# First mLSTM gates worked out among the input projection's tiles, decay products removed, and twelve unused products ahead of the prompt recurrence

## The chip, the cores and the metric

One core of one Trainium2 chip runs the whole program. The metric is the device time of one execution in microseconds (us). Five engines work side by side: TensorE (PE in the profile; PEld is its weight load), VectorE (DVE), ScalarE (ACT), GpSimd (POOL) and SyncE (SP), which here only issues DMAs. Each runs its own instruction stream in order and waits on semaphores; a DMA issue (SPq, ACTq) occupies the queue of the engine that issues it.

## The reference, cut to what matters

The step has an mLSTM layer (mixer A), a feed-forward, shared keys and values, a second attention layer and another feed-forward, for one prompt of 1024 frames and eight running streams of 16 frames. All is fp32. What the change touches is the start of mixer A:

```python
q, k, v, o, ig, fg = jnp.split(xn @ w_in, [...], axis=-1)   # 512, 512, 1024, 1024, 8, 8 columns
li = soft_cap(ig + b_i)                  # 15 * tanh(z / 15), per head and frame
lf = log_sigmoid(soft_cap(fg + b_f))
b = jnp.cumsum(lf, axis=-1)              # within a chunk
dmat = where(causal, b[..., :, None] - b[..., None, :] + li[..., None, :], -inf)
m_t = maximum(b + m, max(dmat)); g = exp(b + m - m_t)
s = einsum('bhtd,bhsd->bhts', q, k) * exp(dmat - m_t[..., None])     # the decay
num = g * einsum('bhvd,bhtd->bhtv', c, q) + einsum('bhts,bhsv->bhtv', s, v)
...
c_new = g_c * c + einsum('bhsv,bhsd->bhvd', ws * v, k)               # the state, chunk to chunk
```

## The kernel before, in words

The 1152 frames (1024 of the prompt, 128 of the running streams) are nine tiles of 128. Each stage is a block of five instruction streams; a stage begins when all five of the one before have ended.

**w_in** (function `linear`, lines 368 to 610). Weights arrive on SP's queue in quarters of a 512-column block (L433); POOL splits each quarter into a high and a low part (L61, L456); TensorE makes three products per 128 rows of the contraction and tile (L499 to L501), `t` over nine tiles inside `b` over six blocks; ScalarE copies each finished tile out of PSUM and issues its store to the scratch `qkvo` in DRAM. Behind the sixth block stand the first gates: 72 products of 128x384 (L510 to L512), whose rows go to DRAM (L440).

**Gates** (`mlstm_gates`, L1255 to L1390). The gate rows come back as 8 partitions (one per head) by 1152 frames, and VectorE and ScalarE work out tanh, log-sigmoid, the cumulative sum, the running maximum and the factors per frame in one chain. TensorE turns the results (L1377 to L1384). Nothing else runs meanwhile.

**Prompt recurrence** (`mlstm`, from L1393; its tiles are named mprompt). Eight tiles, each with four pairs of heads. Per pair TensorE makes: a turn of the next tile (L1554, three per tile), the decay of the pair after next (L1563, L1565, L1566: five products, the mask and the cumulative rows spread over 128 partitions by one-hot weights), the next pair's scores (L1577), the numerator (L1604, L1612) and the state's update (L1620). VectorE adds the frame's own gate to the decay (`argument`, L1756), ScalarE takes its exponential (L1676), VectorE multiplies it into the scores (L1764), ScalarE copies the numerator out (L1711) and VectorE scales the state (L1798). At the second pair of a tile VectorE divides the previous tile's output (L1769 to L1774). SP loads two tiles ahead (L1471 queries and keys, L1475 values). In the second tile ScalarE's queue issues thirteen loads of the running streams' states (L1686 to L1690).

**Running recurrence** (mrun, the same function with one tile), and then a chain of projections that begins with w_out. TensorE's order there is written out by hand: per pair the turn, the decay of the pair after next, the next pair's scores, then this pair's numerator and state.

Of the kernel before, what the change touches and what calls it, by code (L numbers as in the profile page):

```python
# [367 lines left out]
def linear(nc, g, xth, xtl, tag, w, segments, gates=None, **source):  # L368
    BANKS = 3
    wv = w.rearrange("(k p) n -> p k n", p=P)  # L370
    QUARTERS = 4
    HK = KC // QUARTERS
    nb = sum(n for _, n, _, _ in segments)
    with Scope(nc, tag) as s:
        raw = s.sb("raw", [P, 2, HK, CB])
        wh, wl = s.sb("wh", [P, 2, KC, CB], fp32r), s.sb("wl", [P, 2, KC, CB], fp32r)
        if segments[0][2] != "residual":
            stage = s.sb("stage", [P, BANKS, CB])
        normed = [m for _, _, m, _ in segments if isinstance(m, tuple)]
        loaded = [s.sem(f"w_loaded{i}") for i in range(2)]  # L380
        w_split, high_sem = s.sem("w_split"), s.sem("w_high")
        psum_ready, stage_ready = s.sem("psum_ready"), s.sem("stage_ready")
        psum_used = [s.sem(f"psum_used{i}") for i in range(len(segments))]
        stored = [s.sem(f"stored{i}") for i in range(BANKS)]
        psum = [s.ps(f"y{i}", [P, CB]) for i in range(BANKS)]
        if normed:
            gain_small, gain = s.sb("gain_small", [P, B_HD]), s.sb("gain", [P, B_HD])
            squares, ss, rms = s.sb("squares", [P, CB]), s.sb("ss", [P, A_H]), s.sb("rms", [P, A_H])
            gain_loaded, square_done, mean_done, root_done = s.sem("gain_loaded"), s.sem("square"), s.sem("mean"), s.sem("root")
        chain_sem = s.sem("chain")  # L390
        tok = s.brief("tok", [P, Activations.SLOTS, D]) if gates else s.sb("tok", [P, Activations.SLOTS, D])
        if gates:

            gh, gl = s.sb("gh", [P, KC, P], fp32r), s.sb("gl", [P, KC, P], fp32r)
        xt = Activations(nc, g, s, xth, xtl, tok=tok, psum=[s.ps(f"xt{i}", [P, CB]) for i in range(2)], **source)
        if gates:
            g_col, g_n, g_parts, g_bias = gates
            g_raw = s.sb("g_raw", [P, KC, g_n])
            g_out = stage[0:g_n, :, :].rearrange("p a n -> p (a n)")
            g_loaded, g_split, g_ready, g_copied, g_stored = (s.sem(n) for n in ("g_loaded", "g_split", "g_ready", "g_copied", "g_stored"))  # L400
            g_psum = [s.ps(f"g{i}", [P, THIRD]) for i in range(3)]
            if g_bias is not None:
                g_add, g_add_loaded = s.sb("g_add", [g_n, 1]), s.sem("g_add_loaded")

        def each_segment(engine, body, chain=None, when=lambda m: True):

            b0 = 0
            for n, (col0, blocks, mode, target) in enumerate(segments):
                if when(mode):
                    start = chain.n if chain else 0  # L410
                    pairs = blocks // 2
                    run(engine, pairs, lambda i: body(n, i, b0), chain)
                b0 += blocks

        with nc.Block() as block:

            @block.sync
            def _(sp):
                if gates and g_bias is not None:
                    sp.dma_start(g_add[:, :], g_bias.rearrange("(h o) -> h o", o=1)).then_inc(g_add_loaded, 16)  # L420
                if normed:
                    sp.dma_start(gain_small[:, :], normed[0][1].to_broadcast((P, B_HD))).then_inc(gain_loaded, 16)

                xt.load_gain(sp)

                def load(n, i, b0):
                    for par in range(2):
                        b = b0 + 2 * i + par
                        col = segments[n][0] + (2 * i + par) * CB
                        for h in range(QUARTERS):  # L430
                            if h >= 2 or not below(b, 1):
                                wait(sp, w_split, QUARTERS * b + h - 1)
                            sp.dma_start(raw[:, h % 2], wv[:, h * HK:(h + 1) * HK, bass.ds(col, CB)]).then_inc(loaded[h % 2], 16)  # L433

                each_segment(sp, load)
                if gates:
                    sp.dma_start(g_raw[:, :, :], wv[:, :, g_col:g_col + g_n]).then_inc(g_loaded, 16)
                    wait(sp, g_copied, 3)
                    for dst, a, b in g_parts:
                        sp.dma_start(dst, g_out[:, a:b]).then_inc(g_stored, 16)  # L440
                    wait(sp, g_stored, 16 * len(g_parts))

            @block.gpsimd
            def _(pool):
                def split(n, i, b0):
                    for par in range(2):
                        b = b0 + 2 * i + par
                        for h in range(QUARTERS):
                            wait(pool, loaded[h % 2], (2 * b + h // 2) * 16 + 16)
                            if not below(b, 2):  # L450

                                wait(pool, psum_ready, (b - 1) * NT)
                            ks = slice(h * HK, (h + 1) * HK)
                            round_high(pool, g, wh[:, par, ks], raw[:, h % 2]).then_inc(high_sem, 1)
                            wait(pool, high_sem, QUARTERS * b + h + 1)
                            pool.tensor_tensor(wl[:, par, ks], raw[:, h % 2], f32(wh[:, par, ks]), ALU.subtract).then_inc(w_split, 1)  # L456
                            if below(b, 1):
                                xt.scale_gates(pool, h)
                        if below(b, 1):
                            for t in range(QUARTERS, NT):  # L460
                                xt.scale_gates(pool, t)

                each_segment(pool, split)
                if gates:
                    wait(pool, g_loaded, 16)
                    wait(pool, xt.transposed, 2 * NT)
                    pool.memset(f32(gh[:, :, :]), 0.0).then_inc(g_split, 1)
                    pool.memset(f32(gl[:, :, :]), 0.0).then_inc(g_split, 1)
                    wait(pool, g_split, 2)
                    pool.tensor_copy(gh[:, :, 0:g_n], g_raw[:, :, :]).then_inc(g_split, 1)  # L470
                    wait(pool, g_split, 3)
                    pool.tensor_tensor(gl[:, :, 0:g_n], g_raw[:, :, :], f32(gh[:, :, 0:g_n]), ALU.subtract).then_inc(g_split, 1)

            @block.tensor
            def _(pe):
                def products(n, i, b0):
                    for par in range(2):
                        b = b0 + 2 * i + par
                        for t in range(NT):
                            bank = t % BANKS  # L480
                            if below(b, 1):
                                if t == 0:
                                    xt.transpose(pe, 0)
                                    xt.transpose(pe, 1)
                                else:
                                    xt.transpose(pe, t + 1)
                                pe.wait_ge(xt.low_done, 2 * t + 2)
                            if t < BANKS and b0 == 0 and par == 0 and below(i, 1):
                                pass
                            elif t < BANKS and par == 0 and below(i, 1):  # L490

                                pe.wait_ge(psum_used[n - 1], NT * segments[n - 1][1] - BANKS + t + 1)
                            else:
                                pe.wait_ge(psum_used[n], (b - b0) * NT + t - BANKS + 1)
                            for k in range(KC):
                                if t == 0 and k % HK == 0:
                                    pe.wait_ge(w_split, QUARTERS * b + k // HK + 1)
                                xs = slice(t * P, (t + 1) * P)
# [15 lines left out]

            @block.scalar
            def _(act):
                xt.start_act(act)
                xt.high(act, 0)
                xt.high(act, 1)

# [88 lines left out]

class NextTiles:


# [765 lines left out]

# [1411 lines left out]
```

## Time and profile before

| what | us |
|---|---|
| median of three runs | 3531.0 (3496.63, 3531.0, 3543.12) |
| profiled execution | 3529.51 (its span 3528.1) |
| TensorE busy | 3242.7 (92%) |
| mean granted TensorE clock | 0.943 of full speed |
| w_in, from its first product to its last | 17.54 to 342.85 |
| gates stage | 346.4 to 395.0 |
| prompt recurrence, first DMA issue to last state update | 396.2 to 550.1 |
| running recurrence | 562.7 to 626 |

The granted clock is given as a share of full speed: 1.00 is the upper of TensorE's two levels (2.4 GHz), 0.50 the lower (1.2 GHz). Busy time is not useful time: a product at the lower level is busy for twice as long. In a timeline row the bracket says how long the engine had been idle, and for what.

### The profile page before, as it was taken

The numbers are of one execution on the slowest core, as the hardware profiler recorded it, in microseconds if no ns is written. First come the engines' busy times: TensorE is split into PE (matmuls) and PEld (weight loads), VectorE is DVE, ScalarE is ACT, GpSimd is POOL, SyncE is SP. The second block draws the span as 40 slices with busy tenths as digits, with TensorE's granted clock in tenths as the row PEclk, the third lists the DMA queues.
The fourth block names the chain that finished last, engine by engine and source line by source line (L and its number), as shares of the span: only waits on it lengthen the run. The fifth ranks groups of instructions, "written<-read, shape, count | busy, mean of one in ns | idle before, by whom it ended". The sixth has DMA issues, their size and how long they took to land. (4 is left out here: it accounts for less than half of the span.)

```text
span 3528.1 us, 43496 instructions
## 1 busy us (share of the span) xinstructions
PE 3242.7 (92%) x17307; PEld 2797.5 (79%) x17307; DVE 1208.5 (34%) x1913; ACT 608.5 (17%) x1212; POOL 1204.2 (34%) x692
## 2 busy tenths in 40 slices
PE   7998497599999999998999969997779999999999
PEld 6887375479999999986878846665568999999998
DVE  3000433852223332236425135552334233332323
ACT  3111122220000000002111114443313000000000
POOL 4340121452333233423424125662143332234320
PEclk9999567799999999999999969998989999999999
DMA  4221221511111111101222124325651111111111
GB/s 146 96 85 41 58 81 52 173 57 34 60 48 36 36 36 59 36 31 60 93 76 93 63 67 107 93 61 179 220 187 36 48 36 36 36 53 42 48 36 54
DMA packets 177733, 254.44 MB, mean 72 GB/s; under 512 B 33748, under 2 KB 115304, under 8 KB 177608
## 3 DMA queue, kind: packets, MB, share of 16 engines
q1 hardware_dynamic: 137016, 183.19, 16.7%
q10 hardware_dynamic: 38672, 64.27, 5.2%
q0 software_dynamic: 1920, 5.24, 0.4%
q8 instruction: 87, 1.43, 0.2%
q14 instruction: 38, 0.31, 0.0%
HBM read 194.23 MB, written 50.44 MB: 69 GB/s over the span
## 5 line engine op out<-in xcount | busy, mean ns | idle before, releaser
L1081 PE MATMUL A_bank<-A_xth,A_w 128*128 128x384 f32 x1056 | 353.0, 334 | 0.0
L1081 PE MATMUL B_bank<-B_xth,B_w 128*128 128x384 f32 x1056 | 353.0, 334 | 0.0
L1083 PE MATMUL B_bank<-B_xtl,B_w 128*128 128x384 f32 x1056 | 352.9, 334 | 0.0
L1083 PE MATMUL A_bank<-A_xtl,A_w 128*128 128x384 f32 x1056 | 352.9, 334 | 0.0
L1082 PE MATMUL A_bank<-A_xth,A_w 128*128 128x384 f32 x1056 | 352.8, 334 | 0.0
L1082 PE MATMUL B_bank<-B_xth,B_w 128*128 128x384 f32 x1056 | 352.8, 334 | 0.0
L61 POOL TENSOR_TENSOR A_w1h<-A_raw_a,g_one 128x1024 fp32r<-128x1024 f32 (+1 forms) x31 | 79.8, 2574 | 500.1 <-PE A_bank L1109 323.4
L1181 DVE TENSOR_TENSOR g_x<-B_bank,g_x 128x512 f32<-128x512 f32 x198 | 136.9, 692 | 209.7 <-PE B_bank L1109 209.7
L1181 DVE TENSOR_TENSOR g_x<-A_bank,g_x 128x512 f32<-128x512 f32 x198 | 136.2, 691 | 201.9 <-PE A_bank L1109 201.9
L1081 PEld LDWEIGHTS A_bank<-A_xth,A_w 128*128 128x128 f32 x1056 | 198.3, 188 | 0.6 <-issue 0.2
L1081 PEld LDWEIGHTS B_bank<-B_xth,B_w 128*128 128x128 f32 x1056 | 198.3, 188 | 0.6 <-issue 0.2
L1082 PEld LDWEIGHTS A_bank<-A_xth,A_w 128*128 128x128 f32 x1056 | 198.3, 188 | 0.4
L1082 PEld LDWEIGHTS B_bank<-B_xth,B_w 128*128 128x128 f32 x1056 | 198.3, 188 | 0.4
L1083 PEld LDWEIGHTS B_bank<-B_xtl,B_w 128*128 128x128 f32 x1056 | 198.3, 188 | 0.0
L1083 PEld LDWEIGHTS A_bank<-A_xtl,A_w 128*128 128x128 f32 x1056 | 198.3, 188 | 0.0
L499 PE MATMUL w_in_y<-w_in_wh,A_xth 128*128 128x512 f32 x432 | 171.3, 396 | 7.5 <-POOL w_in_wl L456 7.5
L2100 POOL TENSOR_TENSOR fprompt_acc<-fprompt_acc,fprompt_prob 128x512 f32<-128x512 f32 (+3 forms) x160 | 152.4, 952 | 60.7 <-ACT fprompt_prob L2286 44.8
L61 POOL TENSOR_TENSOR B_w1h<-B_raw_a,g_one 128x2048 fp32r<-128x2048 f32 (+1 forms) x15 | 48.1, 3209 | 360.6 <-PE B_bank L1109 323.4
L501 PE MATMUL w_in_y<-w_in_wh,A_xtl 128*128 128x512 f32 x432 | 170.1, 394 | 0.0
L500 PE MATMUL w_in_y<-w_in_wl,A_xth 128*128 128x512 f32 x432 | 170.0, 394 | 0.0
L61 POOL TENSOR_TENSOR A_w<-A_raw_a,g_one 128x1024 fp32r<-128x1024 f32 x42 | 88.7, 2112 | 235.2 <-PE A_bank L873 80.3
L1107 PE MATMUL A_bank<-A_w1h,A_w1l 128*128 128x512 f32 x396 | 156.7, 396 | 12.2 <-issue 7.3
(470 smaller groups left out, 6915.4 us busy)
## 6 DMA issues: line engine op xcount, KB each, us to landing
frun_v<-in_cache_v_dram SPq DMA_DIRECT2D x8, 2048.0 KB, 8.9
qkvo<-w_in_stage ACTq DMA_DIRECT2D x54, 256.0 KB, 2.0
w_in_raw<-in_w_in_a_dram SPq DMA_DIRECT2D x24, 512.0 KB, 3.7
A_raw_b<-in_w_gu_dram SPq DMA_DIRECT2D x11, 1024.0 KB
A_raw_a<-in_w_down_dram SPq DMA_DIRECT2D x11, 1024.0 KB, 4.8
B_raw_b<-in_w_gu_dram SPq DMA_DIRECT2D x11, 1024.0 KB
B_raw_a<-in_w_down_dram SPq DMA_DIRECT2D x11, 1024.0 KB, 4.8
A_raw_a<-in_w_gu_dram SPq DMA_DIRECT2D x10, 1024.0 KB
```

The source lines that it names most:

```text
L61: return pool.tensor_tensor(out, in_, ones, ALU.mult)
L499: pe.matmul(psum[bank][:, :], xth[:, k, xs], wh[:, par, k], start=(k == 0), stop=False)
L500: pe.matmul(psum[bank][:, :], xth[:, k, xs], wl[:, par, k], start=False, stop=False)
L501: ins = pe.matmul(psum[bank][:, :], xtl[:, k, xs], wh[:, par, k], start=False, stop=(k == KC - 1))
L1081: pe.matmul(banks[j][:, :], h[:, f, k], xth[:, k, self.thirds[j]], start=(k == 0), stop=False)
L1082: pe.matmul(banks[j][:, :], l[:, f, k], xth[:, k, self.thirds[j]], start=False, stop=False)
L1083: ins = pe.matmul(banks[j][:, :], h[:, f, k], xtl[:, k, self.thirds[j]], start=False, stop=(k == KC - 1))
L1107: pe.matmul(self.yp[c][:, :], self.hh[:, f, ts], self.dh[:, f, cs], start=(f == 0), stop=False)
L1181: dve.tensor_tensor(xs, self.yp[c][:, :], xs, ALU.add).then_inc(self.added, 1)
L2100: pool.tensor_tensor(to, to, new, ALU.add).then_inc(summed, 1)
```

## The change

`linear` is gone; w_in uses the class `Linear` that four later projections already used, unrolled. It is given a block number at which the gate products stand: 1 here, so they come after block 0 and ahead of block 1. The gate weights are loaded first on SP's queue. A new class `MlstmGates` is a guest of w_in: it works on 64 partitions (head and chunk) by 144 frames, and puts its ScalarE, TensorE and DMA work at fixed (block, tile) places; its cumulative rows go to DRAM. In the recurrences SP loads those rows, broadcast to 128 partitions, for each tile, and VectorE builds the argument from them, the frame's gate and the mask. The five decay products per pair, their PSUM banks and the five casts ahead of them are gone. Ahead of the prompt recurrence's first turn stand twelve products whose result nothing reads.

```diff
 class Linear:
     def sp(self, sp):
+            for a, b, bias in self.g_bias:
+                sp.dma_start(self.g_add[a:b, :], bias).then_inc(self.g_add_loaded, 16)
         for b, (n, bl) in enumerate(self.blocks):
-            if b == 1 and self.gates:
+            if self.gates and b == self.g_block - 2 + (self.g_block == 1):
                 sp.dma_start(self.g_raw[:, :, :], ...).then_inc(self.g_loaded, 16)
...
+            if self.gates and b == self.g_block:
+                sp.wait_ge(self.g_copied, 3)
+                for dst, c0, c1 in self.g_parts:
+                    sp.dma_start(dst, self.g_out[:, c0:c1]).then_inc(self.g_stored, 16)
+                if self.guest:
+                    sp.wait_ge(self.g_stored, 16 * len(self.g_parts))
+                    self.guest.sp_in(sp)
     def pe(self, pe):
-            if last and self.gates:
+            if self.gates and b == self.g_block:
                 self.gate_products(pe)
...
+                if self.guest:
+                    self.guest.pe(pe, b, t)
+class MlstmGates:
+    ROWS = A_H * NP
+    ACT_AT = {(1, 5): "tanh", (1, 7): "exp", (2, 0): "log", (2, 8): "exps"}
+    PE_AT = {(2, 3): "link", (2, 5): "back", (3, 2): "turn"}
...
 def mlstm(...):
+        bb = s.sb("bb", [P, SLOTS, A_H, P])
+        warm = s.ps("warm", [P, CB])
+        WARM = 12
                     sp.dma_start(qk[:, slot], qkvo[t, :, 0:A_V0]).then_inc(qk_loaded[slot], 16)
                     if not below(i, SLOTS):
+                        wait(sp, arg_done, (i - SLOTS + 1) * A_PAIRS)
+                    cols = b_d[:, bass.ds(i * P, P)].rearrange("(o h) n -> o h n", o=1)
+                    sp.dma_start(bb[:, slot], cols.to_broadcast((P, A_H, P))).then_inc(b_loaded[slot], 16)
...
-                def bias(i, slot, j):
-                    pe.matmul(bank[:, :, :], g.ident_r[:, :], mask_r[:, :, :], start=True, stop=False)
-                    for e in range(2):
-                        pe.matmul(bank[:, e, :], g.sel_r[:, 2 * j + e, :], g.Bh[:, cols], start=False, stop=False)
-                        ins = pe.matmul(bank[:, e, :], g.sel_r[:, 2 * j + e, :], g.Bl[:, cols], start=False, stop=(e == 1))
-                    ins.then_inc(bias_ready, 1)
...
-                pe.wait_ge(rounded, 1 if running else 5)
+                if not running:
+                    for n in range(WARM):
+                        pe.matmul(warm[:, :], g.ident[:, :], g.x[:, n % NP, 0:CB], start=True, stop=True)
...
                 def argument(i, slot, j):
-                    dve.wait_ge(bias_ready, i * A_PAIRS + j + 1)
-                    dve.tensor_tensor(arg[:, j], pb[j % 2][:, :, :], spread(tokc[:, slot, KIND_A, 2 * j:2 * j + 2], P), ALU.add).then_inc(arg_done, 1)
+                    if j == 0:
+                        dve.wait_ge(b_loaded[slot], loads(i, slot))
+                    for e in range(2):
+                        h = 2 * j + e
+                        ins = dve.scalar_tensor_tensor(arg[:, j, e, :], bb[:, slot, h, :], tokc[:, slot, KIND_A, h:h + 1], mask[:, e, :], ALU.add, ALU.add)
+                    ins.then_inc(arg_done, 1)
...
-            mlstm_gates(nc, g, gates_d, A["b_i_a"], A["b_f_a"], A["state_m"], m_prompt, m_sample)
+                              gates=(A_O0 + A_H * A_V, 2 * A_H, [...], bias, 1, 3), own=own, guest=gates)
```

On TensorE, before, the gates' last small products are followed by the first turns and the first decay products:

```order
L1377 MATMUL mgates_tok<-g_ident,mgates_en 128x8
L1382 MATMUL mgates_small<-mgates_gend,A_pair_sel 128x8 x4
L1383 MATMUL mgates_small<-mgates_diag,A_ones 128x64
L1384 MATMUL mgates_small<-g_ident,mgates_gend 8x8
L1278 UNCONDITIONAL_BRANCH
L1526 UNCONDITIONAL_BRANCH
L1554 MATMUL mprompt_turn<-g_ident,mprompt_qk 128x128 x8
L1554 MATMUL mprompt_turn<-g_ident,mprompt_qg 128x128 x4
L1563 MATMUL mprompt_bias<-mprompt_mask_r,A_ident_r 128x256
```

With the change, the last products of w_in are followed by the unused ones, and the first pairs have no decay (mprompt_bias):

```order
L642 MATMUL A_bank<-A_w1h,A_xth 128x512
L643 MATMUL A_bank<-A_w1l,A_xth 128x512
L644 MATMUL A_bank<-A_w1h,A_xtl 128x512
L969 UNCONDITIONAL_BRANCH
L1339 UNCONDITIONAL_BRANCH
L1435 MATMUL mprompt_warm<-g_x,g_ident 128x512 x12
L1367 MATMUL mprompt_turn<-g_ident,mprompt_qk 128x128 x8
L1367 MATMUL mprompt_turn<-g_ident,mprompt_qg 128x128 x4
L1378 MATMUL mprompt_scores<-mprompt_qt,mprompt_kt 128x128 x4
L1405 MATMUL mprompt_num_p<-mprompt_v,mprompt_st 128x129 x2
L1413 MATMUL mprompt_num_p<-mprompt_ct,mprompt_qgt 128x129 x2
L1421 MATMUL mprompt_state<-mprompt_wsv,mprompt_k 64x129 x2
```

The gates stage between the two has gone from this place. On SP, before, the w_in weights come first behind the norm's gain, and the gate weights last:

```order
L232 DMA w_in_x_gain<-in_g_mix_dram 128x1024
L433 DMA w_in_raw<-in_w_in_a_dram 128x2x512 x8
L95 UNCONDITIONAL_BRANCH
L433 DMA w_in_raw<-in_w_in_a_dram 128x2x512 x8
L95 REGISTER_ALU
L95 COMPARE_AND_BRANCH
L433 DMA w_in_raw<-in_w_in_a_dram 128x2x512 x8
L437 DMA w_in_g_raw<-in_w_in_a_dram 128x8x16
L440 DMA mlstm_gates_rows<-w_in_stage 16x1152
```

With the change three small loads are ahead of them, and the gates' stores, reloads and old maxima stand between the second and the third block's weights:

```order
L232 DMA A_gain<-in_g_mix_dram 128x1024
L560 DMA A_w_in_g_add<-in_b_i_a_dram 8x1
L560 DMA A_w_in_g_add<-in_b_f_a_dram 8x1
L563 DMA A_gate_raw<-in_w_in_a_dram 128x8x16
L570 DMA A_raw_a<-in_w_in_a_dram 128x2x512 x8
L578 DMA mlstm_gates_prompt<-A_raw_b 16x1024
L578 DMA mlstm_gates_running<-A_raw_b 16x128
L1073 DMA A_gain<-mlstm_gates_prompt 64x128
L1073 DMA A_gain<-mlstm_gates_running 64x16
L1073 DMA A_gain<-mlstm_gates_prompt 64x128
L1073 DMA A_gain<-mlstm_gates_running 64x16
L1075 DMA A_m_prev<-in_state_m_dram 8x1 x8
```

So a transfer of 64 KB in pieces of 16 columns now stands ahead of the first weights, and a wait of SP's stands ahead of the third block's.

## Rows read from the trace of the kernel before

**Rows 1.** Windows by stage: start:end, length, busy us of each engine, granted clock, DMA share, GB/s.

```profile
36.10:330.00 293.90, 293.90 (x1324) 243.91 (x1323) 18.87 (x29) 46.19 (x82) 84.86 (x43) 1.00 0.25 84
343.00:401.00 58.00, 6.21 (x47) 6.05 (x47) 34.52 (x46) 12.20 (x11) 5.82 (x15) 0.53 0.08 17
401.00:510.60 109.60, 104.15 (x461) 77.94 (x461) 30.76 (x83) 24.52 (x55) 23.05 (x16) 0.50 0.34 89
510.60:550.10 39.50, 39.11 (x308) 29.18 (x307) 20.11 (x54) 14.57 (x34) 12.10 (x8) 1.00 0.23 80
```

**Rows 2.** Windows inside the prompt recurrence, same columns.

```profile
460.00:480.00 20.00, 20.00 (x93) 14.80 (x91) 6.31 (x17) 4.86 (x11) 4.41 (x3) 0.50 0.13 41
```

**Rows 3.** Timeline, end of w_in and small gate products: start, length, engine, line, operation.

```profile
342.51 0.34 PE L512 MATMUL w_in_g<-A_xtl,w_in_gh 128*128 128x384 f32 x1
343.39 0.35 SPq L440 DMA_DIRECT2D mlstm_gates_rows<-w_in_stage  x1
346.38 0.34 SPq L1282 DMA_DIRECT2D mgates_li<-mlstm_gates_rows  x1
391.86 1.85 PE L1382 MATMUL mgates_small<-mgates_gend,A_pair_sel 8*128 8x8 f32 x8
```

**Rows 4.** Timeline, start of the prompt recurrence.

```profile
396.20 0.38 SPq L1471 DMA_DIRECT2D mprompt_qk<-qkvo  x1
401.03 1.09 PE L1554 MATMUL mprompt_turn<-g_ident,mprompt_qk 128*128 128x128 f32 x4 [6.79 <-DMA mprompt_qk<-qkvo]
402.89 1.09 PE L1554 MATMUL mprompt_turn<-g_ident,mprompt_qk 128*128 128x128 f32 x4 [0.78 <-ACT mprompt_qt L1681]
411.60 1.23 PE L1604 MATMUL mprompt_num_p<-mprompt_v,mprompt_st 128*128 128x129 f32 x4
```

**Rows 5.** Timeline, one pair of heads at the lower clock level.

```profile
477.61 0.58 PE L1563 MATMUL mprompt_bias<-mprompt_mask_r,A_ident_r 128*128 128x256 f32 x1
479.15 0.80 PE L1577 MATMUL mprompt_scores<-mprompt_qt,mprompt_kt 64*128 64x128 f32 x4
479.88 1.23 PE L1604 MATMUL mprompt_num_p<-mprompt_v,mprompt_st 128*128 128x129 f32 x4
485.44 0.80 PE L1604 MATMUL mprompt_num_p<-mprompt_v,mprompt_st 128*128 128x129 f32 x2
```

**Rows 6.** Timeline, last tile, upper clock level; its last pairs have no decay products.

```profile
540.69 0.39 PE L1563 MATMUL mprompt_bias<-mprompt_mask_r,A_ident_r 128*128 128x256 f32 x1
541.59 0.49 PE L1577 MATMUL mprompt_scores<-mprompt_qt,mprompt_kt 64*128 64x128 f32 x4
542.01 0.71 PE L1604 MATMUL mprompt_num_p<-mprompt_v,mprompt_st 128*128 128x129 f32 x4
544.47 1.22 DVE L1774 TENSOR_TENSOR mprompt_hout<-mprompt_num,mprompt_den 128x1024 f32<-128x1024 f32 x1
544.77 0.71 PE L1604 MATMUL mprompt_num_p<-mprompt_v,mprompt_st 128*128 128x129 f32 x4
546.90 0.68 PE L1604 MATMUL mprompt_num_p<-mprompt_v,mprompt_st 128*128 128x129 f32 x4
```

**Rows 7.** Timeline, ScalarE's queue while it issues the state's loads.

```profile
432.22 9.44 ACTq L1690 DMA_DIRECT2D A_cold<-in_state_c_dram  x8
442.54 1.20 PE L1604 MATMUL mprompt_num_p<-mprompt_v,mprompt_st 128*128 128x129 f32 x4 [3.87 <-ACT mprompt_num L1711]
```

**Rows 8.** Timeline, plain fp32 products 128x512 in the running recurrence.

```profile
610.44 1.02 PE L1653 MATMUL mrun_state<-mrun_wsk,A_own 128*8 128x512 f32 x2
611.39 1.13 PE L1663 MATMUL mrun_turn<-mrun_km,mrun_wsv 128*128 128x512 f32 x2
616.37 2.07 PE L1663 MATMUL mrun_turn<-mrun_km,mrun_wsv 128*128 128x512 f32 x2 [0.20 <-DVE A_cold L1826]
```

**Rows 9.** Timeline, VectorE in the recurrence: the argument now, and a fused operation.

```profile
541.70 0.42 DVE L1756 TENSOR_TENSOR mprompt_arg<-mprompt_bias,mprompt_tokc 128x256 f32<-128x256 f32 x1 [0.55 <-PE mprompt_bias L1566]
543.57 0.35 DVE L1798 SCALAR_TENSOR_TENSOR mprompt_ct<-mprompt_ct,mprompt_gcc,mprompt_state 128x129 f32<-128x129 f32 x1 [0.96 <-PE mprompt_state L1620]
```

More of the change, by code:

```diff
@@ L727, in __init__ @@
         self.bank = [s.ps(f"bank{i}", [P, CB]) for i in range(8)]
+        self.gate_raw = self.raw_b[:, T_ALL:T_ALL + n].rearrange("p (k n) -> p k n", k=KC)
         self.hh = self.w1l[:, T_ALL:(1 + FG) * T_ALL]
         self.w = [(self.w0[:, 0, :], self.w0[:, 1, :]), (self.w1h[:, :], self.w1l[:, :])]
+class FirstMemory:
+    def __init__(self, s):
+        self.xth, self.xtl = s.sb("xth", [P, KC, T_ALL], fp32r), s.sb("xtl", [P, KC, T_ALL], fp32r)
+        self.gate_raw = s.sb("gate_raw", [P, KC, 2 * A_H])
+        self.gate_w = [s.sb(f"gate_w{i}", [P, KC, 2 * A_H], fp32r) for i in range(2)]
+        self.raw_b, self.raw_a = s.sb("raw_b", [P, 2 * D]), s.sb("raw_a", [P, 2 * D])
+        pairs = [[s.sb(f"w{i}{part}", [P, KC * CB], fp32r) for part in "hl"] for i in range(2)]
+        self.w = [(h[:, :], l[:, :]) for h, l in pairs]
+        self.wide, self.gain = s.sb("wide", [P, Linear.BANKS * CB]), s.sb("gain", [P, D])
+        self.bank = [s.ps(f"bank{i}", [P, CB]) for i in range(8)]
 class Linear:
@@ L771, in __init__ @@
             self.g_out = mem.raw_b[0:self.g_n, 0:T_ALL]
-            self.g_psum = [mem.bank[5 + j][:, 0:THIRD] for j in range(3)]
+            self.g_psum = [b[:, 0:THIRD] for b in mem.bank[g_bank:g_bank + 3]]
             names = ("loaded", "add_loaded", "split", "ready", "copied", "stored")
@@ L806, in sp @@
                     sp.dma_start(self.gain_small[:, :], self.normed[0][1].to_broadcast((P, B_HD))).then_inc(self.gain_loaded, 16)
-        if self.then:
-            self.then.load_gain(sp)
-        if self.gates:
-            sp.wait_ge(self.g_copied, 3)
-            for dst, a, b in self.g_parts:
-                sp.dma_start(dst, self.g_out[:, a:b]).then_inc(self.g_stored, 16)
+            if b == self.nb - 1 and self.then:
+                self.then.load_gain(sp)
+            if self.gates and b == self.g_block:
[6 more added lines that the diff above has]
+        if self.guest:
+            self.guest.sp_out(sp)
     def sp_end(self, sp):
@@ L820, in pool @@
             par = b % 2
-            if b == 2 and self.gates:
+            if self.gates and b == self.g_block - 1:
                 pool.wait_ge(self.g_loaded, 16)
@@ L902, in act @@
             last = b == self.nb - 1
-            if last and self.gates:
-                act.wait_ge(self.g_add_loaded, 16)
+            if self.gates and b == self.g_block:
+                act.wait_ge(self.g_add_loaded, 16 * len(self.g_bias))
                 for j in range(3):
@@ L1398, in mlstm @@
+def mlstm(nc, g, qkvo, b_d, h_d, running, c_out, n_out, state_c=None, state_n=None):
     tag = "mrun" if running else "mprompt"
@@ L2681, in build @@
     qkvo = scratch("qkvo", (NT, P, A_O0 + A_H * A_V))
-    gates_d = scratch("mlstm_gates_rows", (2 * A_H, T_ALL))
+    gates_d, b_d = ([scratch(f"{name}_{part}", (rows, n)) for part, n in (("prompt", SEQ), ("running", T_ALL - SEQ))]
+                    for name, rows in (("mlstm_gates", 2 * A_H), ("mlstm_cum", A_H)))
     h_d = scratch("mlstm_h", (NT, P, D))
@@ L2701, in build @@
         setup(nc, g)
-        with Scope(nc, "A1") as s:
-            xth, xtl = s.sb("xth", [P, KC, T_ALL], fp32r), s.sb("xtl", [P, KC, T_ALL], fp32r)
-            linear(nc, g, xth, xtl, "w_in", A["w_in_a"][0],
-                   [(0, 4, "store", lambda b, t: qkvo[t, :, bass.ds(b * CB, CB)]),
-                    (A_O0, 2, "sigmoid", lambda b, t: qkvo[t, :, bass.ds(A_O0 + b * CB, CB)])],
-                   gates=(A_O0 + A_H * A_V, 2 * A_H, [(gates_d, 0, T_ALL)], None), kind="norm", gain_row=A["g_mix"][0:1, :], x_arrives=True)
@@ L2745, in build @@
                           (D, 2, "store", rows(v_prompt, v_sample))],
-                         gates=(2 * D, B_H, [(fgates_p, 0, SEQ), (fgates_s, SEQ, T_ALL)], A["b_f_b"]), made=xkv, raw_free=(ffn0.down_split, ffn0.G),
+                         gates=(2 * D, B_H, [(fgates_p, 0, SEQ), (fgates_s, SEQ, T_ALL)], [(0, B_H, A["b_f_b"].rearrange("(h o) -> h o", o=1))], 3, 5), made=xkv, raw_free=(ffn0.down_split, ffn0.G),
                          w_free=([(ffn0.up_ready, ffn0.ALL)], [(ffn0.down_ready, ffn0.G * ffn0.NY), (xkv.transposed, 2 * NT)]),
```

571 lines of the change are left out of this document (188 added, 383 removed).

## The prediction

> **What bounds the kernel now.** I read the windows by stage first, then the timeline at both ends of the stages that the change touches, and then single pairs of the recurrence at either clock level. The windows show three different limits. From 36.1 to 330 us TensorE is busy for all of 293.90 us at granted clock 1.00, so w_in ends when its products end, and whatever moves in among them is added [rows 1]. From 343 to 401 us TensorE does 6.21 us of work in 58: the gates' chain on VectorE is the end there, with the stage changes and the first load [rows 1]. The prompt recurrence then keeps TensorE busy for 104.15 of 109.60 us at clock 0.50, and for 39.11 of 39.50 at 1.00 [rows 1]. So in the recurrence TensorE is the bound at both levels, and the lower level is nearly three quarters of it. The reader should see that the kernel loses time here twice: 58 us with no products, and 110 us of products at half speed.
>
> **Against what the sum is made.** The profiled execution took 3529.5 us, 1.5 below the median of 3531.0; the three runs lie up to 47 apart, so a part of this stretch, such as the moment at which the clock comes back, may differ from run to run. I name the time at which the last state update of the prompt recurrence ends, 550.1 now [rows 1], and take everything behind it as moved by the same amount.
>
> **Start of w_in.** Three small loads are issued on SP ahead of the first weights. An issue costs about 0.35 us [rows 3], so 1.1 us at least; at most the first weights are held for as long as the first load of the recurrence takes from issue to use, 4.83 us (396.20 to 401.03) [rows 4]. I take 2.5, nearer the issues, because the load is an eighth of that one's size. The Trainium skill ("DMA: Bandwidth & Descriptors", section "Specifications") gives 512 B as the least piece at line rate, and the moved load has pieces of 64 B; no run here shows the load alone, and by that the delay would lie in the upper half of these bounds.
>
> **Gate products and their chain.** The 72 products are the same in number and length, only earlier: nothing won or lost on TensorE. Thirteen small products and transposes of the new class are added among w_in's. The nearest row is 1.85 us for four small products at the lower level (eight records) [rows 3], 0.46 each, so 0.23 at the upper: 13 of them are 3.0 us; bounds 1 (hidden in the pipeline) and 6. The chain on VectorE (34.5 us busy before [rows 1]) lies beside products now: VectorE does 18.87 us in the 293.90 of w_in, ScalarE 46.19 [rows 1]. Its cover is some 240 us of products behind block 0; the third block's weights wait on SP for the gates' store, with most of a block in hand. If that cover failed, the third block would start late; that is a rival below. So the last product of w_in ends at 342.85 + 2.5 + 3.0 = 348.4 (342.51 + 0.34 is its end now [rows 3]).
>
> **The exit of the stage.** From that end to the next stage's first DMA issue is 3.5 us now (342.85 to 346.38) [rows 3]; the last store is larger in the new order, so I take 3.8. The recurrence begins at 352.2, where it now has its first issue at 396.20 [rows 4]: 44 us go.
>
> **The twelve unused products.** A plain fp32 product 128x512 starts 0.95 us after the one before at the upper level (610.44 to 611.39) and lasts 2.07 at the lower, against 1.13 [rows 8]. Twelve are 11.4 us, or at most 22.8. The first load hides 4.83 of it [rows 4], so they cost 6.6 us net, 18 at the worst, and can give back only through the clock. First turn at 363.6 instead of 401.03.
>
> **The opening.** From first turn to first numerator is 10.6 us now, at the lower level, with two pairs' decay [rows 4]. A pair's decay is 1.54 us there (477.61 to 479.15) [rows 5], so 7.5 are left; part of it is ScalarE's copies between turns, which follow no TensorE clock. I take 6.7 at the upper level, 7.5 at the lower.
>
> **A tile of the recurrence.** At the upper level a pair without a turn takes 2.76 us (542.01 to 544.77), of which decay is 0.90 (540.69 to 541.59) [rows 6]: 1.86 remain. Four of these and three turns of about 0.4 (1.09 long at the lower level, with its drain [rows 4]) are 8.6 us. VectorE's own work per pair grows: two fused operations 128x128 in place of one of 0.42 over 256 columns. The nearest row is the fused 128x129 at 0.35 [rows 9], so 0.70 against 0.42; with the scores' product and the state it needs about 1.5 of the pair's 1.86. That fits, except where the previous tile's output is divided: that lump holds a 1.22 us operation, and the one row that shows a pair without decay behind the lump gives 2.13 instead of 1.86 (544.77 to 546.90) [rows 6], with the old argument. With the slower one I add 1.4 per tile (bounds 0.3, from this row, and 2.4, no overlap at all): 10.0 per tile, 80 for eight.
>
> **The stall on ScalarE's queue.** The eight state loads hold it for 9.44 us [rows 7]; the exponentials and copies stand behind them. TensorE idles 3.87 us [rows 7] now, because it had work left at the lower level. Faster products use that work up sooner: I take 8.5 (bounds 3.9 and 9.4).
>
> **The clock.** It is at 1.00 when w_in ends, and after 343 the mean of 0.53 over 58 us says that it fell within about 3.5 us of TensorE's last work [rows 1]. So it will fall in the stall, and perhaps just as the unused products begin. I add 5 us for such stretches (bounds 0 and 35, the next paragraph's rival). By the Trainium skill ("TensorE: Matmul & The Clock Gate", section "HAM oscillation — how this bites in real kernels") it is waits between bursts that throttle TensorE again; that speaks against relying on the unused products, since the stall comes after them. But it would also have the unbroken products of 460 to 480 us at the upper level, and the row says 20.00 of 20.00 us busy at 0.50 [rows 2]; there the measurement decides, and a busy engine is no promise of the upper level.
>
> **The sum.** 363.6 + 6.7 + 80 + 8.5 + 5 = 463.8 for the recurrence's end, against 550.1: 86.3 us. The running recurrence loses four decay groups of at most 1.54; part lies under ScalarE's copies, so 3.5 of 6.2. Together 89.8: 3529.5 - 89.8 = **3440 us**, 2.6% under the median.
>
> **Rivals.** (1) **The lower level stays** through the recurrence, as it did for 110 us under a fully busy engine [rows 1, 2]. A tile is then four pairs of 5.56 (479.88 to 485.44, one of them without its turn) less four decays of 1.54 [rows 5], about 15.3; 7.5 + 8 x 15.3 + 5 of stall = 135, end 499, so 55 us less than now: 3475. For it: rows 2. Against it: the same stream did run at 1.00 for its last 39.5 us [rows 1], and without the decay products, which use 8 rows of the array, what remains is denser. Chance 0.20. (2) **The clock is never lost**, or the lump hides: 3428, chance 0.05. (3) **The gates hold up w_in**: a step of the chain is late at its place and the third block's weights come late; 15 us more, 3455; chance 0.04. (4) **Slower: the loads bound the tiles.** SP's queue now holds queries and keys, the broadcast rows, and values, with two tiles in flight, and values are asked for only when the last numerator of the tile before is done. What is won outside the tiles is 37 + 4 us, so the kernel becomes slower when a tile takes over (149 + 41 - 7.5)/8 = 22.8 us. The first load lands in 4.8 us [rows 4] and DMA share is 0.34 [rows 1], so the broadcast would have to make it over three times as long; at 25 us a tile 3547. Chance 0.03. That the change doesn't do what it says is unlikely: the decay products and the gates stage are absent from the order.
>
> **Numbers.** 3440 with chance 0.68, its own range 3420 to 3460. The range 3418 to 3478 takes in rivals 1 to 3 and the bounds of stall, lump and clock. What a measurement here can tell from no change is about 2%, so faster means below 3460: 0.73, from the main case, (2), most of (3) and a little of (1), whose half-way forms lie on the border; same 0.24; slower 0.03.
>
> **What would show it.** Right: first turn near 364, granted clock near 1.00 in the second half of the recurrence, pairs of 1.9 to 2.5 us, one gap of 8 us on TensorE behind the state loads, recurrence over by 465. Wrong: a gap of TensorE between blocks of w_in; pairs of 3.4 us or more at 0.50; TensorE waiting for DMA at the head of tiles.

## The result, and the profile after

The changed kernel takes 3480.25 us (median of 13 runs, 3467.97 to 3485.37) against 3541.3 for the kernel before (13 runs, 3496.63 to 3553.72): the ratio is 0.9856, 95% interval 0.9827 to 0.9885. It is faster by 1.4%, clear of the noise, but by less than the 2% that the prediction took as the least that a measurement here tells from no change; 2.6% were forecast, and the time lies 2 us above the forecast range. The ratios in this document are worked out from averages that leave out executions in a slower state, as some of the kernel before are, so they differ a little from the quotient of the medians. The profiled execution took 3479.06 us against 3529.51.

The windows by stage of the changed kernel answer to [rows 1]; the columns are the same:

```profile
36.10:330.00 293.90, 293.90 (x1352) 239.77 (x1351) 43.95 (x82) 52.28 (x92) 83.58 (x39) 1.00 0.25 82
346.00:362.00 16.00, 12.03 (x25) 5.21 (x25) 2.18 (x6) 0.60 (x1) 2.12 (x5) 0.89 0.65 143
362.00:369.00 7.00, 2.99 (x21) 2.00 (x19) 0.95 (x3) 3.97 (x7) 3.38 (x2) 0.87 0.72 169
369.00:466.00 97.00, 84.13 (x398) 57.93 (x396) 38.03 (x111) 23.87 (x57) 22.30 (x15) 0.50 0.50 126
466.20:483.30 17.10, 11.85 (x97) 8.24 (x96) 11.33 (x27) 5.09 (x12) 5.36 (x4) 1.00 0.41 115
483.30:504.00 20.70, 19.82 (x96) 13.63 (x96) 9.87 (x25) 5.53 (x14) 4.10 (x5) 0.50 0.06 26
```

The gates' 58 us are gone: w_in is full as before, and 16 us lie between its end and the first turn. But of the recurrence only 17 us ran at 1.00; 97 us and then 20.7 us ran at 0.50. The timeline at the stage's start, for [rows 3, 4]:

```profile
345.61 0.39 PE L644 MATMUL A_bank<-A_w1h,A_xtl 128*128 128x512 f32 x1
349.92 0.37 SPq L1267 DMA_DIRECT2D mprompt_qk<-qkvo  x1
362.04 0.60 PE L1367 MATMUL mprompt_turn<-g_ident,mprompt_qk 128*128 128x128 f32 x4
366.10 1.28 ACT L1474 ACT_TABLE_LOAD   x1
368.32 0.80 PE L1378 MATMUL mprompt_scores<-mprompt_qt,mprompt_kt 64*128 64x128 f32 x4 [2.45 <-DVE mprompt_st L1558]
369.06 1.23 PE L1405 MATMUL mprompt_num_p<-mprompt_v,mprompt_st 128*128 128x129 f32 x4
```

w_in ends at 346.0, the unused products go from 349.97 to 362.04, the first numerator comes at 369.06. In between TensorE waits 2.45 us for VectorE, which waits for the exponential, whose table ScalarE loads only now (1.28 us). In this opening TensorE was busy for 2.99 of 7 us, and its level fell at 367.2. It had fallen once before, at 350.1, behind TensorE's wait of 3.97 us after w_in: the first of the unused products ran at the lower level, and under them it came up again at 353.5:

```profile
350.50:353.50 3.00, 3.00 (x5) 1.15 (x4) 0.50 (x2) 0.00 (x0) 0.50 (x2) 0.50 0.75 213
```

The start of the program, where the gate weights went ahead:

```profile
11.02 0.54 POOL L594 CAST A_gate_w<-A_gate_raw 128x128 fp32r<-128x128 f32 x1 [8.19 <-DMA A_gate_raw<-in_w_in_a_dram]
13.63 1.89 POOL L61 TENSOR_TENSOR A_w0h<-A_raw_a,g_one 128x1024 fp32r<-128x1024 f32 x1 [1.53 <-DMA A_raw_a<-in_w_in_a_dram]
18.09 0.76 PE L642 MATMUL A_bank<-A_w0h,A_xth 128*128 128x512 f32 x1 [2.06 <-POOL A_w0l L609]
```

POOL's first rounding waits until 13.63 for the first weights and the first product begins at 18.09, against 17.54 before.

The state loads, for [rows 7], and then one whole tile at the upper level, for [rows 6]:

```profile
385.91 15.62 ACTq L1488 DMA_DIRECT2D A_cold<-in_state_c_dram  x8
402.41 1.20 PE L1405 MATMUL mprompt_num_p<-mprompt_v,mprompt_st 128*128 128x129 f32 x4 [12.87 <-ACT mprompt_num L1509]
418.51 1.23 PE L1405 MATMUL mprompt_num_p<-mprompt_v,mprompt_st 128*128 128x129 f32 x4
```

```profile
466.58 0.71 PE L1405 MATMUL mprompt_num_p<-mprompt_v,mprompt_st 128*128 128x129 f32 x4
467.89 1.40 DVE L1549 SCALAR_TENSOR_TENSOR mprompt_arg<-mprompt_bb,mprompt_tokc,g_mask_kq 128x128 f32<-128x128 f32 x2
469.69 0.49 PE L1378 MATMUL mprompt_scores<-mprompt_qt,mprompt_kt 64*128 64x128 f32 x4 [1.01 <-DVE mprompt_st L1558]
470.16 0.68 PE L1405 MATMUL mprompt_num_p<-mprompt_v,mprompt_st 128*128 128x129 f32 x4
472.69 0.68 PE L1405 MATMUL mprompt_num_p<-mprompt_v,mprompt_st 128*128 128x129 f32 x4
474.52 0.71 PE L1405 MATMUL mprompt_num_p<-mprompt_v,mprompt_st 128*128 128x129 f32 x4
476.96 0.71 PE L1405 MATMUL mprompt_num_p<-mprompt_v,mprompt_st 128*128 128x129 f32 x4
```

The loads hold ScalarE's queue for 15.62 us, not 9.44, and TensorE idles for 12.87. The whole tile that follows, from 402.41 to 418.51, takes 16.1 us at the lower level. At the upper level the tile from 466.58 to 476.96 takes 10.38 us: a plain pair 1.83 (472.69 to 474.52), one with a turn 2.44 (474.52 to 476.96), and the pair behind the division 3.58 (466.58 to 470.16), 1.01 of which TensorE waits for VectorE. Right behind this tile the upper level is lost again:

```profile
473.98 0.35 ACTq L1492 DMA_DIRECT2D mlstm_h<-mprompt_hout  x1
480.84 1.23 DVE L1568 TENSOR_TENSOR mprompt_hout<-mprompt_num,mprompt_den 128x1024 f32<-128x1024 f32 x1 [3.89 <-DMA mlstm_h<-mprompt_hout]
482.39 1.40 DVE L1549 SCALAR_TENSOR_TENSOR mprompt_arg<-mprompt_bb,mprompt_tokc,g_mask_kq 128x128 f32<-128x128 f32 x2
482.50 1.15 POOL L1308 TENSOR_TENSOR mprompt_qg<-mprompt_qk,mprompt_tokc 128x512 f32<-128x512 f32 x1 [9.94 <-DVE mprompt_tokc L1538]
484.19 0.80 PE L1378 MATMUL mprompt_scores<-mprompt_qt,mprompt_kt 64*128 64x128 f32 x4 [5.13 <-DVE mprompt_st L1558]
```

VectorE waits 3.89 us for the store of the previous tile's output, since there is one buffer for it and the store is issued late on ScalarE's queue (473.98). TensorE has 5.13 us without work, and the next scores run at 0.50.

### The profile page after: what moved, and what is told of

Read it like the earlier page. It is cut to its first block and busy times, and to the rows that moved or that the text cites. A ratio compares the mean times of both kernels' runs of the same rounds, so it can differ in the third digit from the quotient of the medians.

```text
span 3477.6 us, 43151 instructions
## 1 busy us (share of the span) xinstructions
PE 3221.8 (93%) x17126; PEld 2761.2 (79%) x17126; DVE 1226.6 (35%) x1957; ACT 601.4 (17%) x1211; POOL 1199.1 (34%) x682
## 5 line engine op out<-in xcount | busy, mean ns | idle before, releaser
L61 POOL TENSOR_TENSOR A_w1h<-A_raw_a,g_one 128x1024 fp32r<-128x1024 f32 (+1 forms) x43 | 103.9, 2416 | 551.8 <-PE A_bank L886 323.4
L642 PE MATMUL A_bank<-A_w1h,A_xth 128*128 128x512 f32 x576 | 225.4, 391 | 0.0
L644 PE MATMUL A_bank<-A_w1h,A_xtl 128*128 128x512 f32 x576 | 224.2, 389 | 0.0
L643 PE MATMUL A_bank<-A_w1l,A_xth 128*128 128x512 f32 x576 | 224.1, 389 | 0.0
```

The lines of the kernel that those rows point to most:

```text
L61: return pool.tensor_tensor(out, in_, ones, ALU.mult)
L642: pe.matmul(bank[:, :], self.mem.xth[:, k, xs], self.wh[par][:, k], start=(k == 0), stop=False)
L643: pe.matmul(bank[:, :], self.mem.xth[:, k, xs], self.wl[par][:, k], start=False, stop=False)
L644: ins = pe.matmul(bank[:, :], self.mem.xtl[:, k, xs], self.wh[par][:, k], start=False, stop=(k == KC - 1))
```

## The experiments

The first four kernels ran in one group and the next four in a second, on one chip; the last four ran in a third, on another chip. The kernel before ran in each. Its median was 3535.0 in the first group, 3550.5 in the second, 3540.7 in the third; its runs spread by some 50 us, and so the intervals against it are wide. Kernels of one group are compared by their medians. The changed kernel's 3480.25 comes from its own runs, so a difference from it, or between groups, of only some us says little by itself.

**Without the unused products.**

```diff
-        WARM = 12
+        WARM = 0
```

> The changed kernel without its twelve unused products. Theory L (the lower clock level holds through most of the recurrence whatever stands ahead of it; the products bought only some 5 us at the upper level, up to 367.2): first turn comes when the first load has landed, about 355 instead of 362.0, the opening runs at the lower level and takes 1 to 2 us more, so 4 to 6 us less than the changed kernel's 3480: 3475. Rival W (the products do bring the clock, and without them even less of the recurrence is at the upper level): 3485 or more.

Measured 3471.6 us (3467.3 to 3473.1; ratio 0.9847, 0.9783 to 0.9911). The first turn waits for its load alone:

```profile
352.45 1.11 PE L1367 MATMUL mprompt_turn<-g_ident,mprompt_qk 128*128 128x128 f32 x4 [7.88 <-DMA mprompt_qk<-qkvo]
```

352.45 against 362.04. w_in ended 1.4 us earlier in this run (344.6), so the products delayed the first turn by 8.2 us. Theory L holds, W falls: leaving them out is, if anything, better by 8 us, because the level that they held lasted for 5 us of an opening in which TensorE mostly waits.

**State loads on SP's queue.**

```diff
 @block.sync:   chunks(sp, load)
                if not running:
+                    load_running_states()
 @block.scalar:
-                        if j == A_PAIRS - 1 and not running and below(i, 1):
-                            load_running_states()
```

> The changed kernel with the thirteen state loads issued on SP's queue behind its last tile load, not on ScalarE's in the second tile. Theory L: TensorE's gap of 12.87 us at 389 goes and nothing takes its place, the level stays low until about the same point of the recurrence: 3467. Rival S (the gap is what keeps the clock down: without it the stream is unbroken and the upper level comes early): tiles of 10 to 11 us in place of 16, 3440 or less.

Measured 3465.0 us (3462.6 to 3467.3; 0.9828, 0.9765 to 0.9891): 15 us less than the changed kernel, little more than the gap. The window over its recurrence, in the first row, is the clearest of this study:

```profile
367.00:490.00 123.00, 123.00 (x582) 84.77 (x583) 57.30 (x164) 34.64 (x82) 31.73 (x23) 0.50 0.48 120
466.13 9.37 SPq L1284 DMA_DIRECT2D A_cold<-in_state_c_dram  x8
```

TensorE was busy for 123.00 of 123.00 us, without a gap, and all of it at 0.50. A gap is not what holds the level down; S falls. The second row is the eight state loads in their new place, with no broadcast rows on their way: 9.37 us, as in the kernel before. The Trainium skill ("TensorE: Matmul & The Clock Gate", section "HAM oscillation — how this bites in real kernels") tells of waits between bursts that throttle TensorE again; the falls at 367.2 and 483.3 behind waits agree with it, this stretch without any wait is not covered by it.

**Two output buffers.**

```diff
-hout = s.sb("hout", [P, A_H, A_V])
+hout = s.sb("hout", [P, SLOTS, A_H, A_V])      # and one semaphore per buffer
```

> The changed kernel with two buffers for a tile's output, so that VectorE doesn't wait for the store of the tile before. Theory H: the 5.13 us gap at 479 goes, the level does not fall there, the last 20 us run at the upper level and take about 12: 5 + 8 = 13 less, 3467. Rival: the level falls all the same and only 3 to 5 us go (3476), or nothing, since VectorE then waits for the broadcast rows.

Measured 3469.8 us, but 3456.5 to 3484.7 (0.9858, 0.9790 to 0.9926). The profiled execution is the fastest of them, and had two stretches at the upper level:

```profile
417.00:444.00 27.00, 22.25 (x180) 15.59 (x180) 21.46 (x55) 11.05 (x27) 10.38 (x8) 1.00 0.53 173
478.50:489.00 10.50, 9.05 (x77) 6.28 (x76) 5.55 (x16) 3.50 (x9) 0.00 (x0) 1.00 0.13 51
```

```profile
442.95 0.49 PE L1381 MATMUL mprompt_scores<-mprompt_qt,mprompt_kt 64*128 64x128 f32 x4 [1.55 <-DVE mprompt_st L1562]
```

The gap at 479 is gone, and H is borne out for that. But the first stretch ended at 444.3, and in the 8 us before it TensorE had waited for no more than the 1.55 us of this row and 1.37: the level can fall here without a wait of several us. When it comes up and falls differs from run to run of one kernel. The mean granted clock of the four runs goes with their time, from 0.954 at 3456.5 us to 0.942 at 3484.7, and so it does in the kernel before, from 0.952 at 3501.0 to 0.935 at 3546.2. On time alone the run is inconclusive.

**Decay products back, unused.**

```diff
+                def decay():                       # ident_r, mask_r: copies of the identity and the mask
+                    pe.matmul(bank[:, :, :], ident_r[:, :], mask_r[:, :, :], start=True, stop=False)
+                    for e in range(2):
+                        pe.matmul(bank[:, e, :], ident_r[0:A_H, :], mask_r[0:A_H, e, :], start=False, stop=False)
+                        pe.matmul(bank[:, e, :], ident_r[0:A_H, :], mask_r[0:A_H, e, :], start=False, stop=(e == 1))
```

> The changed kernel with the five decay products per pair put back on TensorE as products that nothing reads, in their old place and shapes. Theory L: at the lower level each pair gets 1.54 us longer where TensorE is the bound, at the upper 0.9: 35 to 45 us more, about 3520, so most of the saving came from these products. Rival D (with more products in the stream the upper level comes earlier, as it did at 510 us in the kernel before): 20 us more or less, about 3500.

Measured 3510.5 us (10 runs, 3501.6 to 3515.8; 0.9952, 0.9917 to 0.9986). 30 us more than the changed kernel, between the two expectations: TensorE's gap behind the state loads shrank to 6.5 us, since at this pace it has work for longer, and the rest is decay at the lower level:

```profile
371.00:531.00 160.00, 153.55 (x726) 114.41 (x724) 57.52 (x161) 34.65 (x81) 31.67 (x23) 0.53 0.35 91
```

Four of the five products use 8 rows, and the level did not come up for them (mean 0.53). So, by medians of different groups, about half of the 60 us that the change brought are the decay products.

**No gaps, and a product that is not needed.** With both gaps gone, one unused fp32 product of 128, 256 or 512 columns per pair was put ahead of the numerator:

```diff
+                        if not running:
+                            pe.matmul(warm[:, 0:256], g.ident[:, :], g.x[:, 0, 0:256], start=True, stop=True)
                         numerator(i, slot, j)
```

> The changed kernel with the state loads on SP's queue behind its last tile load and two buffers for a tile's output. Theory L (no gap is what keeps the level low; a stream without gaps stays low until some chance moment): 12.9 less than the changed kernel for the loads, and up to 5 for the store where the level is up: 3460 to 3467. Rival S (the two gaps together hold it down): 3440 or less.

> As the run before with one unused fp32 product 128x128 per pair on TensorE, ahead of its numerator, in the prompt recurrence. Theory F (what keeps the level low is how little of its busy time TensorE's stream computes; some more dense columns bring it up): tiles of about 11 instead of 16 us once it is up, 3440 at best. Theory L (the level doesn't follow what the stream holds): 32 products of about 0.43 at the lower level, 14 us more than without: 3478.

> The same with a product 128x256 per pair. Theory F: the upper level from the second or third tile on, 8 tiles of about 12 us: 3435 to 3445. Theory L: 32 times 0.87 more than without: 3491.

> The same with a product 128x512 per pair, 0.95 us at the upper level and 1.9 at the lower by the running recurrence's rows. Theory F: the upper level nearly throughout, but TensorE is longer busy per pair than VectorE, 1.86 + 0.95 = 2.8 a pair, tiles of 12.5 to 13: 3440 to 3450, a little slower than the half as long products. Theory L: 32 times 1.8 more than without: 3520.

| kernel | median us (range) | ratio to before |
|---|---|---|
| both gaps gone | 3464.2 (3457.4 to 3470.5) | 0.9817 (0.9691 to 0.9943) |
| and 128 columns | 3437.1 (3429.3 to 3446.4) | 0.9727 (0.9600 to 0.9854) |
| and 256 columns | 3441.1 (3439.1 to 3444.8) | 0.9744 (0.9620 to 0.9868) |
| and 512 columns | 3451.9 (3451.2 to 3452.4) | 0.9777 (0.9653 to 0.9901) |

The windows over the recurrence, in the order of the table (for 256 columns the second row leaves the start out):

```profile
367.00:488.00 121.00, 117.41 (x596) 80.85 (x596) 61.15 (x170) 35.40 (x84) 31.85 (x23) 0.56 0.47 127
```

```profile
369.00:466.00 97.00, 88.88 (x642) 64.73 (x642) 62.50 (x164) 34.39 (x84) 31.96 (x23) 0.86 0.54 152
```

```profile
369.00:463.00 94.00, 87.93 (x644) 64.40 (x645) 59.91 (x163) 34.74 (x82) 31.86 (x23) 0.95 0.64 157
378.00:463.00 85.00, 78.93 (x604) 57.98 (x604) 56.92 (x155) 32.54 (x77) 30.72 (x22) 1.00 0.68 166
```

```profile
371.00:474.00 103.00, 99.50 (x651) 63.09 (x649) 62.10 (x162) 34.24 (x82) 31.93 (x23) 0.98 0.55 139
```

Without the product, L's 3460 to 3467 came true and S's 3440 or less did not: with both gaps gone the level was up for 14 us and fell at 387.3, where TensorE had waited 1.35 us at most in the 8 us before. With the product TensorE's granted clock goes from a mean of 0.56 to 0.86, 0.95 and 0.98: work that nobody reads brings the level up, and each kernel is faster than the one that does without. Theory F holds, its sizes to within 3 us. The runs also draw together, from a spread of 17 us with 128 columns to 1 us with 512: little is left to chance there, and the price is then the products themselves.

**The product alone, gaps left in.** The edit above with 128 columns, on the changed kernel.

> The changed kernel with nothing else than one unused fp32 product 128x128 per pair in the prompt recurrence; the state loads stay on ScalarE's queue and the tile's output has one buffer. Theory F (the stream's density sets the level): the level comes up as in the run with the same product and without the two gaps, falls in the 13 us behind the state loads and comes back: 13 + 5 us more than that run's 3437, about 3455. Rival S (it needs the gaps gone as well): 3480 to 3490.

Measured 3479.4 us (3476.1 to 3491.7; 0.9846, 0.9779 to 0.9913), no better than the changed kernel. F's 3455 missed, and S's 3480 to 3490 is what came, to within 1 us:

```profile
384.68 16.29 ACTq L1491 DMA_DIRECT2D A_cold<-in_state_c_dram  x8
401.02 0.42 ACT L1477 ACTIVATE mprompt_arg<-mprompt_arg 128x256 f32<-128x256 f32 x1 [17.91 <-issue]
```

```profile
434.25 0.80 PE L1378 MATMUL mprompt_scores<-mprompt_qt,mprompt_kt 64*128 64x128 f32 x4 [3.99 <-DVE mprompt_st L1561]
481.18 0.80 PE L1378 MATMUL mprompt_scores<-mprompt_qt,mprompt_kt 64*128 64x128 f32 x4 [3.07 <-DVE mprompt_st L1561]
369.00:503.00 134.00, 108.00 (x654) 78.38 (x656) 62.69 (x163) 34.35 (x82) 31.88 (x23) 0.69 0.46 111
```

The level is up for longer (mean 0.69 over the stretch), but at the faster pace the loads hold ScalarE for 17.91 us in all and TensorE for 15.3, and where VectorE waits for the store there are two further gaps, of 4.0 and 3.1 us. In each of the three the level, which was up, fell; the scores behind the two last 0.80 us and not 0.49. So against the changed kernel's 3480.25, across groups, the product alone buys 1 us, taking the gaps out alone 16, and both together 43.

**The same product with 8 rows.**

```diff
-pe.matmul(warm[:, 0:256], g.ident[:, :], g.x[:, ...])
+pe.matmul(warm[:, 0:256], g.ident[0:8, :], g.x[0:8, ...])
```

> As the run with an unused product 128x256 per pair and both gaps gone, but the product uses 8 rows of the array in place of 128, as four of the five decay products did; it lasts as long. Theory R (it is how much of the array works that counts, so these products don't bring the level up): 3464 + 28 = 3490. Rival B (it is how long columns stream, whatever the rows): as with 128 rows, 3441.

Measured 3475.7 us (3470.1 to 3484.2; 0.9828, 0.9761 to 0.9894):

```profile
369.00:503.00 134.00, 132.18 (x646) 84.18 (x644) 59.69 (x162) 34.92 (x82) 31.83 (x23) 0.64 0.43 110
```

By medians of different groups it is 11 us slower than without it and 35 us slower than with 128 rows, so it does not do what the full product does. But the mean of 0.64 is above the 0.56 without it. R is nearer; that rows alone decide is not shown.

**Without the products ahead, with 256 columns per pair.**

> As the run with an unused product 128x256 per pair and both gaps gone (3441), without the twelve products ahead. Theory L: those cost 8 us of delay (first turn 352.4 without them, 360.7 to 362.0 with them) and buy 5 us at the upper level in an opening that mostly waits: 3434. Rival W: the level comes up a few tiles later without them: 3445 or more.

Measured 3430.9 us (3426.7 to 3438.4; 0.9708, 0.9644 to 0.9772), 3 us below what L said, against 3441.1 with them (another group). The level comes up at 370.3, in the first tile, without them:

```profile
363.50:370.00 6.50, 6.28 (x28) 4.58 (x26) 2.34 (x6) 1.40 (x3) 3.37 (x3) 0.50 0.73 188
370.50:457.50 87.00, 80.92 (x624) 59.31 (x622) 56.47 (x155) 32.98 (x79) 30.94 (x22) 1.00 0.63 163
```

**A version meant to beat both.**

```diff
+                act.activation(early[:, :], g.one[:, 0:1], ACT.Exp)     # ahead of the first copy
...
-        WARM = 12
+        WARM = 0
                 for part in range(PARTS):
                     turn(0, 0, part)
+                    unused(2)
                 scores(0, 0, 0)
+                unused(2)
```

> A version meant to beat both kernels: state loads on SP, two output buffers, one unused product 128x128 per pair, no products ahead of the first turn; instead two unused 128x512 behind each of the three turns and two behind the first scores, where TensorE waits for ScalarE, and ScalarE's table for the exponential loaded ahead of the first copy. Theory F: the opening's waits are filled, the level is up by the first tile, 80 to 85 us of recurrence from 362: 3425. If the products lengthen the opening more than they fill: 3435.

Measured 3427.3 us (3424.7 to 3429.0): ratio to the kernel before 0.9688 (0.9625 to 0.9751), the lowest median of all and some 53 us under the changed kernel's, though its runs overlap with those of the kernel just above. The opening, and the recurrence:

```profile
354.00:366.00 12.00, 12.00 (x40) 6.11 (x41) 3.82 (x8) 2.71 (x6) 3.79 (x3) 0.82 0.96 165
365.00:452.00 87.00, 79.06 (x644) 57.88 (x644) 60.41 (x163) 34.14 (x82) 33.55 (x25) 0.98 0.67 177
```

The opening is full, 12.00 of 12.00 us. The first numerator comes at 365.8, 2 us later than in the run before, but from there to the last state update it takes 88 us and not 94. The level is up from the first tile on, where in the run before it came at 370.3, and each pair carries 128 unused columns in place of 256; how much each of the two gives was not told apart.

## Why the prediction was wrong

**Start of w_in, gate products, exit.** Right and a little generous: w_in's last product ended at 346.0, where 348.4 was forecast, the first turn at 362.0 for 363.6. The start was late by 0.55 us (18.09 for 17.54), for which 2.5 had been taken with a lower bound of 1.1: the small pieces cost next to nothing. The gates' chain held nothing up.

**The twelve products.** Sized about right: 12.1 us for 11.4, with the first of them at the lower level, and 8.2 of delay against 6.6. They did bring the level up, at 353.5, but gave nothing back by it: it was lost at 367.2.

**The opening and a tile at the upper level.** 7.0 us for 6.7, and 10.38 us for the one whole tile at the upper level, where 10.0 were forecast. These terms stand.

**The stall.** The step "I take 8.5 (bounds 3.9 and 9.4)" failed: 12.87. Its upper bound was the 9.44 us for which eight of the thirteen issues held the queue; all thirteen held it longer in the kernel before:

```profile
430.27 1.57 ACTq L1686 DMA_DIRECT2D A_nload<-in_state_n_dram  x4
```

From here to the end of the eight, at 441.66, it is 11.4 us. In the changed kernel it is 17.6 us, 15.62 of them for the eight, now that the broadcast rows, with 8.5 us from issue to landing, are on their way in that stretch. With the loads behind all broadcast rows the eight took 9.37 again, which fits; but that run changed queue and place at once, and the connection was not tested apart.

**A gap that was not named.** The store that VectorE waits for, 5.13 us, at the only place where the recurrence had the upper level.

**The clock.** This is the step that failed: "I add 5 us for such stretches". From first turn to last state update it is 142.0 us, where 100.2 were forecast. Opening and stall make 19.9, the store's gap 5.1, and eight tiles at 10.4 would make 83; about 34 us are left, and they are the lower level: a tile takes 16.1 us there, 5.7 more, and about six of the eight ran there. Rival (1) was the case that happened, at a chance of 0.20. That its 3475 is only 5 us short of the result is partly luck: its stall was 7.9 too small and the store's gap of 5.1 was not in it, but its eight tiles together came out 5.4 too long, as more than one of them ran at the upper level, and the start and the opening gave 2.0 back. Its 15.3 for a tile at the lower level was itself 0.8 too small. The reason given against it, that the stream without decay is denser, was not borne out: the stream stayed at 0.50 for 123 us without a gap. [rows 2] had shown just that in the kernel before, and it deserved the greater chance.

**The running recurrence** gave about 4 us for 3.5.

So where did the expected gain go? Not to a new bound: the gates' stage and the decay products paid what they were to pay. The upper level that the twelve products were to hand to the recurrence was lost in the opening, and the recurrence's own stream brought it back only at 466.2, for 17 us. The runs with a product per pair and no gaps show that this is the cause: with the level up for most of the recurrence (mean 0.86 and 0.95) the kernel takes 3437 to 3441 us. That this is where the sum had put it is partly luck, as the sum has 13.5 us for stall and clock in place of these products. Why this stream by itself stays at the lower level, and what in the product lifts it, stays open.

## What to carry to other kernels

A busy TensorE is not at its upper clock for that: read the granted clock beside the busy time of the same window before a stage is priced at its faster rows, and ask what brings the level up there. Products ahead of a stage help only if the stage itself then keeps the level; here a small useless product inside the loop, with no wait of several us around it, was worth more than twelve in front of it. Whoever makes a stage faster should list every buffer and queue that the old pace had hidden: here a store with one buffer made TensorE wait 5.1 us and thirteen DMA issues 12.9, and where the level was up it fell in such a wait. Taking these waits out was not enough, though: with both gone the level still fell, and its mean was 0.56.

## What the runs showed of the hardware

The fused operation that now builds the argument reads two tiles in SBUF. Its row in the changed kernel, with the shortest, the median and the longest in ns:

```profile
L1549 DVE SCALAR_TENSOR_TENSOR mprompt_arg<-mprompt_bb,mprompt_tokc,g_mask_kq x64: 337/346/1401, 360.6 to 497.4; 128x128 f32<-128x128 f32 x64
```

By its timeline, the 44 of them beside which POOL did nothing took 0.345 us on average, and the 20 that overlapped an operation of POOL's took 0.73, up to 1.40; the pair at 482.39 above runs beside POOL's at 482.50. The state's fused operation, which reads one operand from PSUM, took 0.348 (24 of them) and 0.343 (8 that overlapped). The Trainium skill ("SBUF — State Buffer", section "Who interferes with whom") says that a VectorE instruction with two SBUF inputs contends with a GpSimd instruction that reads SBUF, and the trace agrees. At the lower level this hid behind TensorE. At the upper one it is part of the 3.58 us pair behind the division: the two at 467.89 take 1.40 us, ahead of the operation that TensorE waits 1.01 for.
